# Up projection of a feed-forward block: 13 of 22 column pairs by seven block products instead of 9, in straight-line code, with partial sums read out of open PSUM groups by ScalarE

## The reference

```python
h = rmsnorm(x, ffn_norm[l])
u = h @ ffn_w_up[l]                    # [512, 1024] @ [1024, 5632]
a, bv = u[..., :D_FF], u[..., D_FF:]   # D_FF = 2816 = 22 * 128
a = causal_dwconv(a, ffn_conv_w[l], ffn_conv_b[l])   # 3 taps along the sequence
x = x + (jax.nn.silu(a) * bv) @ ffn_w_down[l]
```

## Time and profile before

| what | value |
|---|---|
| three runs, median | 1963.65 us |
| lowest, highest | 1961.56, 1965.49 us |
| profiled execution, first to last instruction | 1959.6 us |
| TensorE busy | 99% of the span |
| VectorE busy | 65% |
| ScalarE busy | 45% |
| up projection, layer 0, TensorE on pairs 3 to 21 | 289.27 to 488.82 us |

### The profile page before, as it was taken

How to read it: one execution, slowest core, us unless ns; L and a number is a source line. 1 busy time by engine, 2 the same in 40 slices (tenths; PEclk the granted TensorE clock), 3 DMA queues, 4 the chain that set the end, 5 groups by cost and what they waited for, 6 DMA issues and landing times.

```text
span 1959.6 us, 30739 instructions
## 1 busy us (share of the span) xinstructions
PE 1937.3 (99%) x11610; PEld 1631.9 (83%) x11610; DVE 1276.2 (65%) x1564; ACT 875.9 (45%) x1281; POOL 30.0 (2%) x60
## 2 busy tenths in 40 slices
PE   7999999999999999999999999999999999999998
PEld 5887889898887897889898888997777777888888
DVE  6866788887656866788877646846664644534435
ACT  5345453444323345453344322344445666544343
POOL 2001000000000001000000000000000000000000
PEclk9999999999999999999999999999999999999999
DMA  7213133333324213133333223533332222232322
GB/s 197 87 39 105 44 108 101 92 107 102 102 76 126 74 49 108 44 108 89 104 98 111 94 84 97 173 82 98 85 112 67 61 82 65 87 118 76 100 88 82
DMA packets 241075, 182.38 MB, mean 93 GB/s; under 512 B 12970, under 2 KB 232360, under 8 KB 240574
## 3 DMA queue, kind: packets, MB, share of 16 engines
q1 hardware_dynamic: 238368, 177.37, 30.7%
q0 software_dynamic: 2160, 2.22, 0.6%
q10 hardware_dynamic: 430, 1.23, 0.2%
HBM read 168.21 MB, written 2.10 MB: 87 GB/s over the span
## 4 chain that ended last, share of the span: by engine, by line
PE 89%; DVE 6%; issue 2%; ACT 1%; DMA 1%; DVEq 0%; SPq 0%; POOL 0%; ACTq 0%
PE ps L881 19%; PE ps L883 19%; PE ps L882 19%; PE ps L1420 4%; PE ps L1419 4%; PE ps L1418 4%; PE ps L668 2%; PE ps L644 2%; PE ps L657 2%; DVE amat L2238 2%; PE ps L1318 1%; PE ps L1317 1%; PE ps L1316 1%; PE ps L520 1%; PE ps L489 1%
## 5 line engine op out<-in xcount | busy, mean ns | idle before, releaser
L881 PE MATMUL ps<-h_hi,w_hi 128*128 128x512 f32 (+1 forms) x1232 | 477.1, 387 | 1.1 <-ACT qk L1623 0.7
L883 PE MATMUL ps<-h_hi,w_lo 128*128 128x512 f32 (+1 forms) x1232 | 468.0, 380 | 0.0
L882 PE MATMUL ps<-h_lo,w_hi 128*128 128x512 f32 (+1 forms) x1232 | 465.6, 378 | 0.0
L2124 DVE TENSOR_TENSOR w_lo<-w_raw,w_hi 128x2048 fp32r<-128x2048 f32 (+3 forms) x110 | 227.0, 2063 | 147.1 <-ACT w_hi L1630 142.1
L881 PEld LDWEIGHTS ps<-h_hi,w_hi 128*128 128x128 f32 x1232 | 231.6, 188 | 51.1 <-issue 8.0
L883 PEld LDWEIGHTS ps<-h_hi,w_lo 128*128 128x128 f32 x1232 | 231.4, 188 | 44.4
L882 PEld LDWEIGHTS ps<-h_lo,w_hi 128*128 128x128 f32 x1232 | 231.6, 188 | 43.8 <-issue 1.9
L1630 ACT ACTIVATE w_hi<-w_raw 128x2048 fp32r<-128x2048 f32 (+3 forms) x108 | 186.7, 1729 | 180.2 <-PE ps L1420 124.9
L2632 DVE TENSOR_TENSOR w_lo<-w_raw,w_hi 128x1024 fp32r<-128x1024 f32 (+1 forms) x118 | 126.5, 1113 | 155.6 <-ACT w_hi L1951 154.8
L881 PE MATMUL ps<-w_hi,h_hi 128*128 128x256 f32 x544 | 152.4, 280 | 0.3 <-DVE h_lo L855 0.3
L882 PE MATMUL ps<-w_lo,h_hi 128*128 128x256 f32 x544 | 150.7, 277 | 0.0
(11 more groups left out here) (437 smaller groups left out, 3469.8 us busy)
## 6 DMA issues: line engine op xcount, KB each, us to landing
w_raw<-in_ffn_w_up_dram SPq DMA_DIRECT2D x88, 512.0 KB, 4.5
w_raw<-in_w_in_dram SPq DMA_DIRECT2D x41, 1024.0 KB, 5.3
w_raw<-in_w_in_dram SPq DMA_DIRECT2D x32, 512.0 KB, 5.2
w_raw<-in_ffn_w_down_dram SPq DMA_DIRECT2D x32, 512.0 KB, 4.3
w_raw<-in_w_out_dram SPq DMA_DIRECT2D x12, 1024.0 KB, 5.2
w_raw<-in_ffn_w_down_dram SPq DMA_DIRECT2D x16, 384.0 KB, 3.6
swapped<-qk SPq DMA_DIRECT2D x96, 64.0 KB, 2.0
w_raw<-in_w_mem_kv_dram SPq DMA_DIRECT2D x4, 1024.0 KB, 5.1
```

The lines of the kernel that those rows point to most:

```text
L881: pe.matmul(dst, lh, rh, start=first and j == 0, stop=False)
L882: pe.matmul(dst, lh, rl, start=False, stop=False)
L883: ins = pe.matmul(dst, ll, rh, start=False, stop=last and j == len(order) - 1)
L2124: dve.tensor_tensor(w_lo[:, slot, 0:n], w_raw[:, slot, 0:n], w_hi[:, slot, 0:n].bitcast(F32), ALU.subtract).then_inc(sem("w_split"), 1)
```

## The change

The loops are gone: all 22 pairs are straight-line code on TensorE, ScalarE and VectorE (the loop over the two layers and SyncE's loop stay). Pairs 3, 5, 6, 7, 9, 10, 11, 13, 14, 15, 17, 18, 19 are fast, that is 13 of 22: after pair 5, three fast pairs and then a plain pair.

A fast pair's products are ordered anew. Four of them add up, one after the other, in one open PSUM group ("chain"), and ScalarE copies the sum out three times on the way (`keep` 1, 3 and 4), between two products of the group; two more share the value's first half, with one copy between them (`keep` 2, from PSUM to PSUM). TensorE waits for each copy (`kept`). What is left on VectorE is one addition of 256 columns (`first_gate`), the scaling (`gate_fast`) and one addition of 512 columns (`value_fast`). `s_hi` and `s_lo` are made in two instructions each, of 1024 and 512 columns, the second when the third sum's product is through. The four weight sums stand at the end of the round before.

```diff
+PLAIN_F = (0, 1, 2, 4, 8, 12, 16, 20, 21)
+FAST_F = tuple(f for f in range(KF) if f not in PLAIN_F)
@@ TensorE, fast_pair
-product(pe, part(5, 0), block(0, 1), tokens_(0, 0), range(4)).then_inc(sem("p1_done"), 1)
-product(pe, part(2, 1), block(4, 1), tokens_(4, 0), range(4))
-pe.wait_ge(sem("t_split"), upto(pe, "t_split", 4))
-product(pe, part(4, 0), block(0, 0), mixed_t(2), range(4))
-product(pe, part(4, 1), block(4, 0), mixed_t(3), range(4))
-pe.wait_ge(sem("s_split"), upto(pe, "s_split", n + 1))
-product(pe, part(3, 0), summed(1), mixed_t(1), range(4))
-product(pe, part(3, 1), summed(0), mixed_t(0), range(4)).then_inc(sem("tile_done"), 1)
-product(pe, part(2, 0), summed(2), tokens_(4, 1), range(4)).then_inc(sem("tile_done"), 1)
+product(pe, chain, block(0, 1), tokens_(0, 0), range(4), last=False, read_open=True).then_inc(sem("part_done"), 1)
...
+pe.wait_ge(sem("s_split"), upto(pe, "s_split", 2 * n + 1))
+product(pe, part(value, 0), summed(0), mixed_t(0), range(4), last=False, read_open=True).then_inc(sem("part_done"), 1)
+kept(1)
+product(pe, chain, summed(1), mixed_t(1), range(4), first=False, last=False, read_open=True).then_inc(sem("part_done"), 1)
+kept(2)
+pe.wait_ge(sem("s_split"), upto(pe, "s_split", 2 * n + 2))
+product(pe, part(value, 0), summed(2), tokens_(4, 1), range(4), first=False, read_open=True).then_inc(sem("part_done"), 1)
+kept(3)
+product(pe, chain, block(0, 0), mixed_t(2), range(4), first=False, last=False, read_open=True).then_inc(sem("part_done"), 1)
+product(pe, part(value, 1), block(4, 1), tokens_(4, 0), range(4), read_open=True).then_inc(sem("tile_done"), 1)
+kept(4)
+product(pe, chain, block(4, 0), mixed_t(3), range(4), first=False, read_open=True).then_inc(sem("tile_done"), 1)
@@ ScalarE
+for f in range(3, KF + 1):
...
+        keep(f, 1, 1, hid[:, f, 256:512], chain)
+        conv_start(f - 1, (f - 1) % 2)
+        keep(f, 2, 2, part(4 + 2 * s, 0), part(2 * s + 1, 0))
+        next_up_high(f)
+        keep(f, 3, 3, hid[:, f, 0:256], chain)
+        if f + 1 in FAST_NO:
+            sums_high(f + 1, 0, 2)
+            sums_high(f + 1, 2, 3)
+        keep(f, 4, 5, c_sum[:, s], chain)
+        conv_silu(f - 1)
@@ VectorE
+for f in range(3, KF + 1):
+    if f - 1 in FAST_NO:
+        gate_fast(f - 1)
+        value_fast(f - 1)
+    else:
+        gate_tile(f - 1, (f - 1) % 2)
+    if f < KF:
+        split_low(C_UP + f + 1, (f + 1) % 2, KD)
+    conv_taps(f - 1, (f - 1) % 2)
+    if f + 1 in FAST_NO:
+        sums_low(f + 1, 0, 2)
+        sums_low(f + 1, 2, 3)
+    if f in FAST_NO:
+        first_gate(f)
+    if f - 1 in FAST_NO:
+        hidden_fast(f - 1)
+    else:
+        hidden(f - 1, plain((f - 1) % 2))
+    if f + 2 in FAST_NO:
+        weight_sums(f + 2)
```

More of the change, by code:

```diff
@@ L872, in normed, with product @@
             return full
-        def product(pe, dst, lhs, rhs, order, first=True, last=True, ready=None):
+        def product(pe, dst, lhs, rhs, order, first=True, last=True, ready=None, read_open=False):
             for j, k in enumerate(order):
@@ L880, in product @@
                     pe.wait_ge(sem("h_lo"), upto(pe, "h_lo", ready + j + 1))
-                pe.matmul(dst, lh, rh, start=first and j == 0, stop=False)
-                pe.matmul(dst, lh, rl, start=False, stop=False)
-                ins = pe.matmul(dst, ll, rh, start=False, stop=last and j == len(order) - 1)
+                pe.matmul(dst, lh, rh, start=first and j == 0, stop=False, skip_group_check=read_open)
+                pe.matmul(dst, lh, rl, start=False, stop=False, skip_group_check=read_open)
+                ins = pe.matmul(dst, ll, rh, start=False, stop=last and j == len(order) - 1, skip_group_check=read_open)
             return ins
@@ L1404, in _ @@
+                    kept(4)
+                    product(pe, chain, block(4, 0), mixed_t(3), range(4), first=False, read_open=True).then_inc(sem("tile_done"), 1)
+                up_tile(0, 0)
+                sum_stat(pe, 8)
+                up_tile(0, 1)
+                for f in range(1, KF):
+                    if f in FAST_NO:
+                        fast_pair(f)
+                    else:
+                        for half in range(2):
+                            up_tile(f, half)
                 count["tile_done"] = 2 * C_DOWN
@@ L1892, in _ @@
-                with act.Fori(0, FAST - 1) as n:
-                    fast_act(n)
-                    sums_high(2 * n + FAST_FROM, n + 1)
-                fast_act(FAST - 1)
-                up_high(FAST_TO, 1)
-                for f in (FAST_TO + 1, FAST_TO + 2):
-                    conv_start(f, f % 2)
-                    conv_silu(f)
-                    up_high(f, f % 2)
-                    for k in range(8 * (f - FAST_TO - 1), 8 * (f - FAST_TO)):
+                sums_high(3, 0, 2)
+                sums_high(3, 2, 3)
@@ new lines, in _ @@
+                for f in range(3, KF + 1):
+                    s = f % 2
+                    part = lambda bank, c: ps[:, bank, c * 256:c * 256 + 256]
+                    if f in FAST_NO:
+                        chain = part(5 + 2 * s, 1)
+                        if f == 19:
+                            act.wait_ge(sem("s_split"), upto(act, "s_split", 2 * FAST_NO[f] + 1))
+                        keep(f, 1, 1, hid[:, f, 256:512], chain)
[8 more added lines that the diff above has]
+                        conv_silu(f - 1)
+                    else:
+                        if f < KF:
+                            next_up_high(f)
+                        conv_start(f - 1, (f - 1) % 2)
+                        if f + 1 in FAST_NO:
+                            sums_high(f + 1, 0, 2)
+                            sums_high(f + 1, 2, 3)
+                        conv_silu(f - 1)
+                        if f == KF:
+                            next_up_high(f)
+                    for k in range(8 * (f - KF + 1), 8 * (f - KF + 2)) if f >= KF - 1 else ():
@@ L2545, in _ @@
                 block_low(1)
[L2546 to L2547 removed]
+                weight_sums(3)
                 gate_tile(1, 1)
@@ L2573, in _ @@
-                fast_even(FAST - 1)
-                gate_fast(FAST_TO, FAST - 1)
-                conv_taps(FAST_TO, 1)
-                hidden_fast(FAST_TO, FAST - 1)
-                split_low(C_UP + FAST_TO + 2, 1, KD)
-                for f in (FAST_TO + 1, FAST_TO + 2):
-                    gate_tile(f, f % 2)
-                    conv_taps(f, f % 2)
-                    hidden(f, plain(f % 2))
-                    split_low(C_UP + f + 2, f % 2, KD)
-                    for k in range(8 * (f - FAST_TO - 1), 8 * (f - FAST_TO)):
+                sums_low(3, 0, 2)
```

191 lines of the change are left out of this document (88 added, 103 removed).

## The result

The changed kernel takes 2009.85 us (median of 4 runs, 2009.02 to 2012.80), the kernel before 1963.73 (median of 4, three of them the runs known before): ratio 1.0235, 95% interval 1.0216 to 1.0254. It is 46 us slower. The prediction said slower, at 1993 us with 1966 to 2008 as its range; the time is 17 us above the forecast and 2 us above the range.

A forecast was written before the change was run, and what follows sets the result against it. TensorE was taken to bound the kernel before, and ScalarE-VectorE order the runs of three after. On the 1959.6 us span, -8.2 + 37.6 = +29.4 gave 1989.0, plus 4.05 to the median, 1993 us; range 1966 to 2008.

The forecast's parts named there:

- The bound: Pairs 3 to 21: TensorE bounds them before; after, ordered ScalarE and VectorE work takes 12.9 us against TensorE's 9.97.
- TensorE stays the bound: Rival for the fast pairs: no wait decides; 1955.4 us, or 1943 with faster matmuls; chance 0.12.
- TensorE's work, -8.2 us: Four more fast pairs a layer, eight in all, each 1.03 us shorter than a plain pair: -8.2 us.
- the ring of 12.9 us: ScalarE and VectorE steps from `keep` 2 of one fast pair to the next's, summed start to start: 12.9 us.
- A run of three: Three fast pairs such as 5, 6, 7: loses 1.4 + 2.9 + 0.4 = 4.7 us; eight runs, +37.6 us.
- The "bounds": Forecast's own range: slower ScalarE-VectorE hand-overs +12 us, 2005; VectorE prices 5% too long -12 us, 1981.
- The first pair, 1.4 us: First of three fast pairs: TensorE gets `keep` 2 0.7 us late and `keep` 3 another 0.7 late.
- The third pair: Last of three fast pairs: no weight sums in its round, 10.35 us of ordered work, so 0.4 us lost.
- The clock's rival: Rival: waits drop TensorE to the 1.2 GHz level for one fast pair a run, +46 us, 2039 us; chance 0.05.
- "0.1 us or less between starts and ends": Words quoted as the prediction's; the prediction text given does not contain them.
- What the prediction said would show it wrong: Fast pairs at 10.0 us, VectorE's previous gate through within 2 us mid-run, or granted clock off 1.00 in 289-505 us.
- the 4.05 us between span and median: Whole kernel: the median of the runs stands 4.05 us above the profiled span, added to 1989.0 for 1993 us.

The follow-up runs named there:

- experiment 1: The changed kernel with the old choice of fast pairs (3, 5, ..., 19, every other one plain): 1962.23 us, ratio 0.9996.
- experiment 2: The changed kernel with ScalarE's `w_hi` right behind the first copy, then the second copy, then `conv_start`: 1983.01 us, ratio 1.0103.
- experiment 5: The changed kernel with ScalarE's `conv_start` moved behind `w_hi` and `keep` 3, and VectorE's weight sums straight behind `hidden`, ahead of `first_gate`: 1973.23 us.
- experiment 7: The changed kernel with VectorE's loop over the two layers written out, so semaphore thresholds are constants; order of work the same: 1994.10 us, ratio 1.0158.
- experiment 3: The changed kernel with one more VectorE addition of 128x512, result unused, ahead of each set of weight sums in the pairs' loop: 2022.49 us.
- experiment 12: The changed kernel with twelve fast pairs in twos, both engines' orders as in experiment 5, and VectorE's layer loop written out: 1962.93 us, ratio 1.0000.
- experiment 11: The kernel before the change with nothing but VectorE's loop over the two layers written out: 1964.02 us, ratio 1.0006.
- number 9: The kernel of experiment 6 with VectorE's loop over the two layers written out: 1958.13 us, ratio 0.9981 to the kernel before.
- experiment 6: The changed kernel with twelve fast pairs, never more than two behind one another, and ScalarE's order as in experiment 2: 1965.84 us, ratio 1.0014.

## Why the prediction came out as it did

- **The bound.** Right: the change makes a ring through ScalarE and VectorE the bound in the runs of three, and nowhere else (experiment 1). Order, not load, is what costs (experiments 2 and 5). The rival on the other side, TensorE stays the bound, is refuted by the 33.9 us of waits for ScalarE's copies.
- **TensorE's work, -8.2 us.** Consistent with the sum; it was not measured apart. Fast pairs without a wait take 9.75 to 9.98 us. The formula that the prediction took from the Trainium skill (TensorE: Matmul & The Clock Gate, "Back-to-back issue gap") is given there for an isolated matmul, not for a stream with a weight load ahead of each; here 119 and 229 ns were measured against its 109 and 216.
- **The step that failed: the ring of 12.9 us.** It measured 13.48, and it was mis-sized, not misplaced. A run of three lost 6.8 us instead of 4.7: of the 2.1 us, 1.0 lies in the first pair, 0.6 in the middle one and 0.5 in the third. The prediction took its prices from rows and its hand-overs from the earlier trace rows, and counted nothing between two instructions of the same engine. There were 0.30 us ahead of `s_lo` and 0.19 ahead of the sums, and experiment 7 takes both away (and 0.09 us between `w_hi` and `w_lo`), and 15.8 us of the whole with them. By the windows: the first pair loses 1.02 us less, the middle 0.34, the third 0.43; 1.79 for a run, 14.3 for eight. The rest, 1.5 us, is no more than noise: the kernel before was 1.0 us faster in that session too. The "bounds" looked for it in the wrong place, between ScalarE and VectorE, and at +12 us gave 2005.
- **It could have been read before.** The trace of the kernel before has the same gap, behind a weight sum and ahead of a tap. Two register instructions stand in it (302.09 and 302.23 us, between the sum's end at 302.06 and the tap at 302.34), one for the threshold of `conv0` and one on the tap's own line. By the taps' line:

```profile
  DVE s_raw L2498: 4.6, 16
```

That is sixteen times 0.29 us, once in each turn of the loop. It cost nothing there, since TensorE waited for nothing. The prediction took a price from the very rows around it (300.65 and 301.37) and passed over it.

- **The first pair, 1.4 us.** Measured 2.4 (12.36 - 9.97); with the loop written out 1.4 (11.34 - 9.97). Its wait for `keep` 2 is 1.60 us where 0.7 was predicted, and 0.75 with the loop written out. Two rounds with sums lead up to it, so it pays the gaps twice; its waits for `keep` 3 are 0.3 us, predicted 0.7. The third pair: 0.9, predicted 0.4, written out 0.5.
- **The clock's rival** (2039 us, chance 0.05) did not happen in the change, whose longest such wait is 1.6 us. It happened in part in experiments 2 and 3. The rule that it drew on, from the Trainium skill (TensorE: Matmul & The Clock Gate, "HAM oscillation"), that work broken by waits can fall back to 1.2 GHz again and again, does hold in those two traces: for 3 us behind a wait, with 5 of 8 and 9 of 16 waits, and in none of the other traces, whose waits for ScalarE in this stage are at most 1.6 us. The page's own example has waits of 3 to 5 us, longer than any predicted or measured here, so the prediction read it too broadly when it said that by that rule the rival would hold.
- **"0.1 us or less between starts and ends"** held for each instruction. What the prediction said would show it wrong (fast pairs at 10.0 us, a gate through within 2 us, a low clock) did not occur. Of the 4.05 us between span and median, about 1.8 is what lies outside the span (1.8 in the change, 1.75 to 2.15 in the experiments); the other 2.2 or so mean that the profile of before is of an execution below the median. As a step from that span to a median the sum is right.

Still open: why the eight runs differ by up to 0.4 us (36.7 to 37.1), and the short stops of experiment 12, which no sum here foresaw.

## What to carry to other kernels

When two engines pass work back and forth, sum the ring from start to start, in program order, and compare it with the bound engine's time for the same piece; busy shares say nothing on it. In that sum look at the brackets between two instructions of the same engine too: thresholds computed from a loop's register, behind a wait for the engine's own last result, cost 0.2 to 0.3 us here at each place, about 0.09 for each instruction; nothing while there was slack (experiment 11), and 15.8 us of the whole when the ring was closed (experiment 7). A long instruction that others wait for goes as early as its inputs allow: with twelve fast pairs, `w_hi` behind copy 1 gave 1958 us (number 9) and behind copy 2 gave 1963 (number 12, whose VectorE order differs too; the two were not told apart by runs).

## What the hardware showed that was not expected

- TensorE's clock fell to the 1.2 GHz level (granted 0.50) for 3 us behind 5 of 8 waits of 1.8 to 2.05 us and behind 9 of 16 waits of 1.85 to 2.68 us, in the midst of a stage otherwise at 2.4 GHz, and behind none of the waits of up to 1.6 us. In experiment 2 each such stretch made its run of three 1.5 to 1.8 us longer; in experiment 3, where TensorE waited again in the next pair, about 0.2.
- The pace of 256-column matmuls with plain weights has two values, 0.118 and 0.113 us, that is 1.41 or 1.36 us for a product of 12 at a granted clock of 1.00; products with the weight sums ran at 0.120, 1.44 us. In experiments 6 and 9 nearly all plain-weight products in the stage ran at 1.36 us; in the change most ran at 1.41 (nearly nine in ten in layer 0). For the 12 pairs of experiment 9 this is up to 0.2 us a pair (9.75 against 9.97). It often turned to 1.41 behind a wait for `keep` 3, and to 1.36 in a plain pair, but not only there; the cause was not looked for.
- An addition of 128 x 512 on GpSimd took 1.3 us at its fastest and up to 3.3. Beside it VectorE's tap took up to 1.78 us and 1.15 in the mean (0.75 before), its subtraction of 2048 columns 2.42 in the mean (2.29); `s_lo`, which does not run beside the sums, kept its 1.22.
